# Key pages from another queue, first tiles loaded a stage earlier, a first tile in halves, and scores moved ahead of a group's products

## The reference, cut to what matters

```python
def indexer_topk(iq, iw, ik_all, q_pos, k_top):
    dots = jnp.einsum('bqhd,bld->bqhl', iq, ik_all) * IDX_DIM ** -0.5
    score = jnp.einsum('bqhl,bqh->bql', jax.nn.relu(dots), iw * IDX_HEADS ** -0.5)
    ...
def dilated_group_attend(q, k_rows, v_rows, q_rows, dilation, n_steps):
    key_rows = q_rows[:, None] - dilation * jnp.arange(n_steps + 1)[None, :]
    valid = key_rows >= 0
    ...
    s = jnp.einsum('bqhd,bqjhd->bqhj', q, k) * HEAD_DIM ** -0.5
    s = jnp.where(valid[None, :, None, :], s, -jnp.inf)
    lse = jax.nn.logsumexp(s, axis=-1)
    p = jnp.exp(s - lse[..., None])
    return jnp.einsum('bqhj,bqjhd->bqhd', p, v), lse
```

## Time and profile before

| what | us |
|---|---|
| median of 3 runs | 1845.66 |
| lowest and highest run | 1841.85, 1846.47 |
| the profiled execution, its own time | 1837.1 |
| its span, first to last instruction | 1835.3 |
| TensorE busy | 1483.1 (81%) |
| VectorE busy | 1085.2 (59%) |
| ScalarE busy | 682.4 (37%) |
| GpSimd busy | 315.4 (17%) |

### The profile page before, as it was taken

One profiled execution on the slowest core, in us unless ns is written; L12 is line 12 of the kernel. 1 busy time (PEld: TensorE's weight loads), 2 busy tenths in 40 slices (PEclk: granted clock), 3 DMA queues, 4 the chain that ended last, 5 costly groups with the idle time before them and its releaser, 6 DMA issues. The chain is left out here.

```text
span 1835.3 us, 26264 instructions
## 1 busy us (share of the span) xinstructions
PE 1483.1 (81%) x8937; PEld 1104.1 (60%) x8953; DVE 1085.2 (59%) x2196; ACT 682.4 (37%) x1338; POOL 315.4 (17%) x265
## 2 busy tenths in 40 slices
PE   3998776979979868887589999879970799999930
PEld 1886324868767734555479999834440577677710
DVE  2542754898888946676652322244542677777748
ACT  2211544464455324444241001111210566666634
POOL 0110772222222100000300000014323111010031
PEclk8998557999989969899779999989985899999975
DMA  8220336566555564512711010242106478972244
GB/s 341 62 79 12 98 131 224 178 223 211 196 181 199 172 225 167 143 44 40 295 55 64 31 63 31 74 188 80 46 26 207 141 280 321 365 297 102 83 164 171
DMA packets 81010, 275.81 MB, mean 150 GB/s; under 512 B 14365, under 2 KB 48608, under 8 KB 70160
## 3 DMA queue, kind: packets, MB, share of 16 engines
q1 hardware_dynamic: 63752, 175.92, 27.5%
q0 software_dynamic: 12416, 81.83, 13.0%
q10 hardware_dynamic: 4752, 16.91, 2.3%
HBM read 238.24 MB, written 80.37 MB: 174 GB/s over the span
## 5 line engine op out<-in xcount | busy, mean ns | idle before, releaser
L1176 DVE TENSOR_SCALAR_CACHE_REDUCE hits<-scores,search_ints 128x384 bf16<-128x384 f32 (+2 forms) x192 | 171.2, 941 | 1.8 <-DVE search_ints L1172 0.6
L2675 DVE TENSOR_TENSOR w_moe_rest<-w_moe,w_moe_high 128x1024 fp32r<-128x1024 f32 x128 | 151.5, 1220 | 20.5 <-ACT w_moe_high L2603 17.3
L2109 PE MATMUL ps<-w_o,mix 128*128 128x512 f32 x288 | 131.0, 616 | 18.9 <-DMA w_o<-w_o 18.9
L123 PE MATMUL ps<-h_high,w_mix_high 128*128 128x344 f32 x384 | 126.1, 328 | 19.2 <-DVE h_t_rest L2004 19.2
L2603 ACT CAST w_moe_high<-w_moe 128x1024 fp32r x128 | 131.4, 1046 | 15.3 <-PE ps L125 10.5
L124 PE MATMUL ps<-w_b_rest,hb_high 128*128 128x512 f32 (+1 forms) x384 | 130.9, 341 | 0.0
L124 PE MATMUL ps<-h_t_rest,w_mix_high 128*128 128x344 f32 x384 | 124.4, 324 | 0.0
L125 PE MATMUL ps<-h_high,w_mix_rest 128*128 128x344 f32 x384 | 124.2, 323 | 0.0
L2018 DVE TENSOR_TENSOR prod<-sig,ps 128x688 f32<-128x688 f32 x24 | 20.9, 871 | 170.8 <-ACT sig L1987 170.8
L2568 PE MATMUL ps<-w_moe,moe_hid_t 128*128 x256 | 115.1, 592 | 1.3 <-ACT moe_y L2622 1.3
L2109 PEld LDWEIGHTS ps<-w_o,mix 128*128 128x128 f32 x288 | 56.2, 197 | 88.4 <-issue 69.1
(11 more groups left out here) (444 smaller groups left out, 3572.7 us busy)
## 6 DMA issues: line engine op xcount, KB each, us to landing
w_moe<-w_moe SPq DMA_DIRECT2D x16, 2048.0 KB, 9.2
win_s<-win POOLq DMA_DIRECT2D x16, 1279.4 KB, 6.6
w_ada_late<-w_ada_late SPq DMA_DIRECT2D x16, 1024.0 KB, 5.0
w_moe<-w_moe SPq DMA_DIRECT2D x16, 1024.0 KB, 10.5
slot_rows<-moe_y ACTq DMA_DIRECT2D x32, 512.0 KB, 8.2
w_mix<-w_mix SPq DMA_DIRECT2D x10, 1408.0 KB, 5.9
xb<-x_tiles SPq DMA_DIRECT2D x24, 512.0 KB, 5.3
win_s<-win POOLq DMA_DIRECT2D x8, 1535.2 KB, 7.0
```

What stands on the lines that cost most here:

```text
L123: nc.tensor.matmul(out, w_high, x_high, start=start, stop=False)
L1176: ch.do(dve.tensor_scalar(hits[j % 2][:, 0:w], k.scores[:, k.score_off[j]:k.score_off[j] + w], level[:, j:j + 1].bitcast(F32), 0.0, ALU.is ...
L2109: last = nc.tensor.matmul(bank(k, 2 * u + c), mix[u][:, kk, :], w_o[:, kk, c * 512:(c + 1) * 512], start=kk == 0, stop=kk == KD - 1)
L2675: dve.tensor_tensor(w_lo[:, c, :], w[:, bass.ds(at + c * UW, UW)], w_hi[:, c, :].bitcast(F32), ALU.subtract)\
```

## The change

Half 7 of the keys is fetched by SyncE behind half 5, instead of gathered by GpSimd; the row numbers for the gather shrink to half 6. SyncE loads the first two x tiles of the dilated stage within the index stage, once `sum_taken` says that the index keys' buffer is free, into that buffer; it waits for them before its barrier. In the dilated stage the first tile is made in halves: ScalarE modulates and casts K slices 0 to 3, VectorE modulates 4 to 7 and subtracts both halves' rests; GpSimd begins with tile 1. At n = 8 and n = 16 TensorE runs the scores of tile n - 1 and the values of tile n - 2 ahead of the query/key products instead of behind them. Some buffers change their addresses.

```diff
@@ stage_index_scores
-    kt_loaded.update({h: k.pool_semaphore(f"keys_t_gathered{h}") for h in (6, 7)})
+    kt_loaded.update({6: k.pool_semaphore("keys_t_gathered6"), 7: S("keys_t_loaded7")})
+    k.xb_at = (sb.offsets["index_keys_t"] + 1023) // 1024 * 1024
+    k.xb = [nc.alloc_sbuf_tensor_at(f"xb{u}", [P, KD, P], F32, offset=k.xb_at + 4 * D * u) for u in range(2)]
...
             fetch_pages(k, sp, kt[5], 16 * 5, 0, 16, kt_loaded[5])
-            for h in (3, 4, 5):
+            fetch_pages(k, sp, kt[7], 16 * 7, 0, 16, kt_loaded[7])
+            for h in (3, 4, 5, 7):
                 sp.wait_ge(kt_loaded[h], 16 * 16)
...
             sp.wait_ge(sum_taken, 1)
+            for u in range(2):
+                sp.dma_start(k.xb[u][:].rearrange("p k t -> p (k t)"), ins["x_tiles"][u]).then_inc(xb_loaded, 16)
             sp.dma_start(k.score_d[:, 0:PAST].rearrange("b (j c) -> b j c", j=4), rows32[:]).then_inc(scores_stored, 16)
             sp.wait_ge(scores_stored, 32)
+            sp.wait_ge(xb_loaded, 32)
...
-            for h in (6, 7):
-                for i in range(16):
-                    pool.indirect_dma_start(kt[h][:]...
+            for i in range(16):
+                pool.indirect_dma_start(kt[6][:]...
@@ stage_dilated, SyncE
-            load(0)
-            load(1)
             sp.dma_start(k.w_b[2][:], ins["w_b"][2]).then_inc(w2_loaded, 16)
@@ TensorE
-                pe.wait_ge(h_ready, n + 1)
+                change = n and n % NT == 0
+                if change:
+                    scores(n - 1)
+                    values(n - 2)
                 if n:
+                    pe.wait_ge(h_ready, n)
                     pe.wait_ge(qk_taken, n)
                 for kk in range(KD):
-                    if n and n % NT == 0:
+                    if n == 0 and kk % HALF == 0:
+                        pe.wait_ge(first_rest, kk // HALF + 1)
+                    if change:
                         pe.wait_ge(w_rest, (n // NT - 1) * KD + kk + 1)
                     last = products(n, QK, 0, 512, kk)
                 last.then_inc(qk_done, 1)
-                if n >= 1:
+                if n >= 1 and not change:
                     scores(n - 1)
-                if n >= 2:
+                if n >= 2 and not change:
                     values(n - 2)
@@ ScalarE
-            modulate(0)
-            high_part(0)
+            for kk in range(HALF):
+                last = nc.scalar.activation(ht[0][:, kk, :], xt[0][:, kk, :], ACT.Identity, bias=sh[:, kk, :], scale=sc[:, kk, :])
+            last.then_inc(first_raw, 1)
+            act.wait_ge(first_raw, 1)
+            nc.scalar.copy(ht_hi[0][:, 0:HALF], ht[0][:, 0:HALF]).then_inc(first_high, 1)
+            act.wait_ge(second_raw, 1)
+            act.sem_inc(h_raw, 1)
+            nc.scalar.copy(ht_hi[0][:, HALF:KD], ht[0][:, HALF:KD]).then_inc(h_high, 1)
             modulate(1)
             high_part(1)
@@ GpSimd
-            rest_part(0)
             rest_part(1)
@@ VectorE
+            for kk in range(HALF, KD):
+                last = dve.tensor_scalar(ht[0][:, kk, :], xt[0][:, kk, :], sc[:, kk, :], sh[:, kk, :], ALU.mult, ALU.add)
+            last.then_inc(second_raw, 1)
+            dve.wait_ge(first_high, 1)
+            dve.tensor_tensor(ht_lo[0][:, 0:HALF], ht[0][:, 0:HALF], ht_hi[0][:, 0:HALF].bitcast(F32), ALU.subtract).then_inc(first_rest, 1)
+            dve.wait_ge(h_high, 1)
+            dve.tensor_tensor(ht_lo[0][:, HALF:KD], ht[0][:, HALF:KD], ht_hi[0][:, HALF:KD].bitcast(F32), ALU.subtract).then_inc(first_rest, 1)
```

More of the change, by code:

```diff
@@ L672, in _ @@
                                             bass.IndirectOffsetOnAxis(ap=ik_rows[:, b, j:j + 1], axis=0)).then_inc(ik_loaded, 16)
-            for h in (6, 7):
-                for i in range(16):
-                    pool.indirect_dma_start(kt[h][:].rearrange("p b c -> p (b c)")[:, i * P:(i + 1) * P], None, ins["pool_kt"],
-                                            bass.IndirectOffsetOnAxis(ap=kt_rows[:, h - 6, i:i + 1], axis=0)).then_inc(kt_loaded[h], 16)
+            for i in range(16):
+                pool.indirect_dma_start(kt[6][:].rearrange("p b c -> p (b c)")[:, i * P:(i + 1) * P], None, ins["pool_kt"],
+                                        bass.IndirectOffsetOnAxis(ap=kt_rows[:, i:i + 1], axis=0)).then_inc(kt_loaded[6], 16)
             pool.wait_ge(ik_loaded, 16 * 4 * NS)
-            for h in (6, 7):
-                pool.wait_ge(kt_loaded[h], 16 * 16)
+            pool.wait_ge(kt_loaded[6], 16 * 16)
         @block.tensor
@@ L796, in _ @@
             dve.wait_ge(small_loaded, 16 * 6)
-            dve.scalar_tensor_tensor(kt_rows[:].rearrange("p h j -> p (h j)"), kt_page[:].rearrange("p h j -> p (h j)"), float(P),
-                                     kt_part[:].broadcast_to([P, 32]), ALU.mult, ALU.add).then_inc(ik_rows_ready, 1)
+            dve.scalar_tensor_tensor(kt_rows[:], kt_page[:], float(P), kt_part[:].broadcast_to([P, 16]), ALU.mult, ALU.add).then_inc(ik_rows_ready, 1)
             dve.scalar_tensor_tensor(ik_rows[:].rearrange("p b j -> p (b j)"), ik_page[:].rearrange("p b j -> p (b j)"), float(ID),
@@ L884, in stage_dilated @@
     prefix = k.thresholds[:, 0:NT - 2]
-    xt = [sb(f"xb{u}", [P, KD, P]) for u in range(2)]
+    xt = k.xb
     ht = [sb(f"hb{u}", [P, KD, P]) for u in range(2)]
@@ L891, in stage_dilated @@
     vb = [sb(f"vb{r}", [P, BH, HD]) for r in range(3)]
-    probs = [sb(f"probs_b{u}", [P, BH, 2 * P]) for u in range(2)]
-    probs_t = [sb(f"probs_bt{u}", [P, BH * 2, P]) for u in range(2)]
+    probs = [sb("probs_b0", [P, BH, 2 * P])]
     part = [sb(f"part{u}", [P, 264]) for u in range(2)]
@@ L896, in stage_dilated @@
     tmp2 = sb("tmpb2", [P, 8, ROT])
+    assert sb.off <= k.xb_at
+    sb.off = k.xb_at + 2 * 4 * D
+    probs.append(sb("probs_b1", [P, BH, 2 * P]))
+    probs_t = [sb(f"probs_bt{u}", [P, BH * 2, P]) for u in range(2)]
     hits = [sb(f"hits{u}", [P, T - (1 - u) * P], BF16) for u in range(2)]
@@ L917, in stage_dilated @@
     w2_loaded = S("w_b2_loaded")
+    first_raw, second_raw = S("hb_first_raw"), S("hb_first_raw_dve")
+    first_high, first_rest = S("hb_first_high"), S("hb_first_rest")
+    HALF = KD // 2
     dve_chain = S("dve_chain_b")
@@ L1092, in modulate @@
             def modulate(n):
-                act.wait_ge(x_loaded[n % 2], 16 * (n // 2 + 1))
                 if n >= 2:
+                    act.wait_ge(x_loaded[n % 2], 16 * (n // 2))
                     act.wait_ge(v_done, n - 1)
@@ L2933, in lay_out @@
     ins["page_list"] = halves.reshape(1, -1)
-    ins["key_page"] = np.ascontiguousarray(np.broadcast_to(halves[6:8], (P, 2, 16)))
+    ins["key_page"] = np.ascontiguousarray(np.broadcast_to(halves[6], (P, 16)))
     ins["key_part"] = np.arange(P, dtype=np.int32)[:, None]
```

4 lines of the change are left out of this document (3 added, 1 removed).

## The result

The changed kernel takes 1818.44 us (median of 5 runs, 1817.27 to 1824.91) where the kernel before takes 1843.83 in the same series (1836.98 to 1846.47): a ratio of 0.9876, 95% interval 0.9851 to 0.9900, or 22.9 us less by that ratio (18.4 to 27.5). Forecast were 22.1 us and 1823.6. The table further down takes the stages around the change apart. One execution of the last experiment took 4094.7 us and is left out of the times given there.

The account below looks back on a forecast made before the run. TensorE was taken to set the pace in both stages, with gains where it stands still. Gains of 9.5, 7.3 and 5.3 sum to 22.1 us, from the median 1845.7 to 1823.6 us; range 1817 to 1833.

Parts of the forecast that it names:

- Half 7 by SyncE: End of index stage: SyncE's pages at 1.04 us each remove TensorE's 9.52 us gather wait; gain 9.5 us.
- half 7 has landed 4.9 us ahead of TensorE: Index stage: SyncE's pages for half 7 land by about 263.5, TensorE finishes half 6 at about 268.4.
- What is late next: Barrier ending the index stage: VectorE through at 272.5, second x tile landed at 272.2, so the tiles cost nothing.
- The rival of late tiles: Barrier ending the index stage: SyncE's wait for the tiles' landing holds it by 2.7 us, giving 1826.3; chance 0.08.
- The signs of being wrong: First product later than 280, half 7 still waiting for `keys_t`, or longer `probs_b` waits in tiles after 8 and 16.
- Pages that do not come earlier: Index stage rival: transfers, not issue, set the pages' pace; half 7 still holds TensorE, 12.6 left, 1833.1; chance 0.04.
- Start of the dilated stage: Barrier to first dilated product: early tile loads and shared halves shorten 10.46 us to 3.2; gain 7.3 us.
- Change of weights: Tiles 8 and 16: scores and values moved into TensorE's wait leave the path; gains 3.4 and 1.9 us.
- the rival in which VectorE takes both back: Dilated stage: VectorE takes back the weight changes' 5.3 us, leaving 16.8 and 1828.9; chance 0.14.
- The clock: After holes it starts low; if it stays up there, 3.1 us more at the most, 1820.5; chance 0.08.
- the other side's case: Dilated stage: the clock stays low after the new start; all eight tiles of a group give 1862; chance 0.04.
- The sum: Whole kernel: 9.5 + 7.3 + 5.3 = 22.1 us gained, forecast 1823.6 us.

Follow-up runs that it names:

- the last experiment: Changed kernel with earlier casts, no SyncE wait for the tiles, SyncE's order changed, and unread products in TensorE's three holes: 1807.18 us, ratio 0.9828; second series 1811.00, 0.9833.
- three others: Kernel before with one part each, GpSimd's gathers kept: x tiles loaded early (1834.83 us), first tile in halves (1832.50 us), scores and values ahead (1833.03 us).
- the second trace: The changed kernel itself, unaltered, measured and traced once more: 1818.21 us, ratio 0.9872 to the kernel before.
- the first trace: The changed kernel's first profiled execution, 1821.75 us; median of its runs 1818.44 us, ratio 0.9876 to the kernel before.
- SyncE's changed order: Changed kernel with earlier casts, no SyncE wait for the tiles, half of half 5's pages issued before w_b, page waits last, slot_scores copied sooner: 1816.55 us, ratio 0.9852.
- the search edit: Changed kernel with VectorE leaving two search pieces of tiles 7 and 15 to the tile behind: 1820.85 us, ratio 0.9897 to the kernel before.
- the extra products: Changed kernel with unread TensorE products, 6 ahead of the first dilated tile and 20 ahead of tiles 8 and 16: 1817.26 us, ratio 0.9865 to the kernel before.

## Why the prediction was right, point by point

**Half 7 by SyncE**, 9.5: the size holds against the trace it was taken from (9.5, and 8.3 in the other trace), but in part by luck: that trace's last gather was issued 1.7 us later than in three others, against which the stage won 6.5 to 9.6. The path of the step does not hold in the two traces of the changed kernel. The page time of 1.04 us was 1.09, and the start was later: SyncE's `w_b` load hangs on TensorE's third key half, whose clock the prediction took as it was in its one trace, and went out 50.3 us behind the stage's start instead of 48.6, so the pages ended at 86.3 and not at 83.1. The step "half 7 has landed 4.9 us ahead of TensorE" failed: the pages had landed some 1.7 us ahead (267.87 + 1.4 = 269.3, against 271.03) in one trace, and held TensorE in the other. That half 7's products also wait for the copy of `slot_scores` is not in the prediction; in the second trace the pages cost 1.1 us beyond it.

**What is late next**: counted from the stage's start, the prediction put VectorE's end at 93.4 us, the tiles' landing at 93.1 and the dilated stage's first instruction at 94.1. VectorE was through at 93.2 and 92.9. In the first trace its own scores (until 273.74) and half 7, through ScalarE's cast (until 273.76), ended its chain together. The tiles went out not behind the copy of `slot_scores` but behind the landing of half 7's pages, at 88.3 and 89.5 instead of 87.3, so SyncE was later than VectorE by some 0.6 us in the first trace, where the barrier opened at 94.1 as forecast, and by some 2 in the second (95.3): VectorE stood 0.96 and 2.44 us at the barrier, against 0.40 in the trace of SyncE's changed order, whose stage it ends itself. The rival of late tiles, given 0.08 and 2.7 us, is thus there in part, through the pages rather than the tiles' flight. In the trace of the search edit, whose third key half ran at the high clock, the step went as the prediction had it.

**The signs of being wrong**: two of the three that the prediction named did show, both small. `keys_t` is what half 7 waits for in the second trace (1.1 us of the 3.69 are its own), and tile 18 waits 1.47 us longer for `probs_b`.

**Pages that do not come earlier**: fallen. SyncE's pages and GpSimd's ran side by side, and the DMA share of 246 to 268 rose from 0.17 to 0.28 (the same stretch from the stage's start, 248.44 to 270.44, has 0.24):

```profile
246.00:268.00 22.00, 22.00 (x70) 6.26 (x64) 13.97 (x15) 12.46 (x23) 4.46 (x5) 0.50 0.28 79
...
410.00:500.00 90.00, 85.38 (x652) 71.74 (x651) 82.51 (x226) 47.92 (x147) 22.19 (x18) 1.00 0.60 206
```

By the Trainium skill (DMA: Bandwidth & Descriptors, Issuing engines are not separate DMA queues) a second issuer saves only issue time, usually small; here issue time was what half 7 waited for, and the measurement decides.

**Start of the dilated stage**, 7.3: 7.37, the same in every trace with both parts (3.08 to 3.10 us), half of it from each.

**Change of weights**, 3.4 and 1.9: 3.38 and 1.87 at their places. At tile 8 nothing is given back (90.25 before and after). At tile 16 about 1 us is, so the rival in which VectorE takes both back is true for a fifth of the 5.3. VectorE's 81.56 of 90 us was the warning; it is 82.51 after.

**The clock**: it came up within the first tile, so the other side's case is out, and it did start low, so the 3.1 us left as an upper end were real: with the extra products the pieces are 2.4 to 3.3 us shorter.

**The sum**: 22.1 forecast, 22.9 (18.4 to 27.5) by the ratio, 20.8 and 18.6 in the two traces. The forecast of 1823.6 lies 5.2 above the measured median; 1.8 of that is the median of before, which came out lower in the larger series, and the rest lies within the interval.

## What to carry to other kernels

Where many small transfers are needed, count what one issue costs its queue, spread the issues, and then follow the new issuer's whole list to the barrier: here SyncE's pages, behind a load that waits for another engine, became the end of the stage in the changed kernel's traces, and a reordering that put issues which wait for nothing into that wait took SyncE off the end. When traces are compared, count from the stage's start, and ask what clock the rows that a forecast stands on ran at. Here VectorE, busy 82.5 of 90 us, handed work put off to it back as a wait one tile later. When TensorE stands still by necessity, products that nobody reads can keep its clock up or bring it back up, as long as they end before the real ones are due.

## What was not expected of the hardware

In the same kernel the clock of the index stage's last tile differs from execution to execution: key halves took 1.94 us in one trace (granted clock 0.50 from 246 to 268, TensorE busy throughout) and 1.07 in the next. The third key half, earlier in the stage, took 1.94 us at 0.50 in both of these traces and 1.07 at 1.00 in that of the search edit, and what hangs on it moved by 2.6 to 3.9 us. One wait of 2.28 us in the settled dilated stage was followed by 12 us at a granted clock of 0.72, and the piece was 5.5 us longer. The score rows, 64 KB, issued behind the two tiles, kept SyncE waiting 3.5 us after their issue.
